# Scaling the rows of the v projection on GpSimd, with weight splits, addends and restores moved

## The reference, cut to what matters

```python
def chunk_mlp_mixer(h, w_uv, ln_gain, ln_bias, ws, bs, w_out):
    z = gelu(einsum('btd,de->bte', h, w_uv))
    u, v = z[..., :C_WIDTH], z[..., C_WIDTH:]
    v = layer_norm(v, ln_gain, ln_bias)
    ...
    mixed = einsum('gts,bnsgc->bntgc', w, vc) + bs[:, :L].T[None, None, :, :, None]
    y = u * mixed.reshape(B, T, C_WIDTH)
    return einsum('bte,ed->btd', y, w_out), v

def conv_ffn(h, conv_hist, w_in, conv_w, conv_b, w_out):
    a, gate = proj[..., :D_FF], proj[..., D_FF:]
    conv = conv_b + sum(full[:, j:j + T] * conv_w[j] for j in range(CONV_W))
    y = einsum('btf,fd->btd', gelu(conv) * gate, w_out)
```

## Time and profile before

| | |
|---|---|
| median of 3 runs | 2880.27 us |
| the profiled execution, its time | 2880.13 us |
| its span, first to last instruction | 2878.4 us |
| mean granted TensorE clock | 0.995 |
| PE busy | 2828.3 us, 98% of the span |
| DVE busy | 1494.2 us, 52% |
| ACT busy | 699.4 us, 24% |
| POOL busy | 740.2 us, 26% |
| PE in the chain that ended last | 92% |

### The profile page before, as it was taken

One profiled execution on the slowest core, in us unless ns is written; L12 is line 12 of the kernel. 1 busy time (PEld: TensorE's weight loads), 2 busy tenths in 40 slices (PEclk: granted clock), 3 DMA queues, 4 the chain that ended last, 5 costly groups with the idle time before them and its releaser, 6 DMA issues.

```text
span 2878.4 us, 44387 instructions
## 1 busy us (share of the span) xinstructions
PE 2828.3 (98%) x16227; PEld 2753.0 (96%) x16227; DVE 1494.2 (52%) x2670; ACT 699.4 (24%) x1157; POOL 740.2 (26%) x549
## 2 busy tenths in 40 slices
PE   8998999999999999999999999999999999999999
PEld 8998889999999999999888999999999999999997
DVE  4558886544444444456422765456544444444452
ACT  4423344311111111113322221214311111111123
POOL 3133334432222222222100330012422222222220
PEclk9999999999999999999999999999999999999999
DMA  4111001111111111111211111111111111111111
GB/s 144 37 33 49 23 17 41 46 42 44 40 43 41 40 43 40 44 40 45 70 44 33 60 41 40 44 40 37 48 45 40 44 40 43 40 43 41 42 53 76
DMA packets 194883, 130.72 MB, mean 45 GB/s; under 512 B 8859, under 2 KB 186724, under 8 KB 194532
## 3 DMA queue, kind: packets, MB, share of 16 engines
q1 hardware_dynamic: 194788, 129.44, 14.8%
HBM read 120.60 MB, written 8.81 MB: 45 GB/s over the span
## 4 chain that ended last, share of the span: by engine, by line
PE 92%; DVE 5%; issue 2%; ACT 1%; POOL 0%; DMA 0%; DVEq 0%; SPq 0%; ACTq 0%; POOLq 0%
PE bank L693 47%; PE bank L718 21%; PE bank L1206 7%; PE bank L742 3%; PE bank L850 3%; PE bank L1130 2%; PE bank L1317 2%; PE bank L881 1%; PE bank L792 1%; PE bank L1098 1%; PE bank L1266 1%; PE bank L1326 1%; DVE qsc L1488 1%; DVE sct L1508 1%; DVE work L1995 0%
## 5 line engine op out<-in xcount | busy, mean ns | idle before, releaser
L2730 POOL TENSOR_TENSOR raw<-raw,vec 128x512 f32<-128x512 f32 x248 | 281.2, 1145 | 1308.1 <-DMA raw<-in_w_in_ffn 845.1
L693 PE MATMUL bank<-xh,wh 128*128 128x384 f32 x2664 | 607.6, 335 | 3.1 <-DVE wl L1345 2.4
L693 PE MATMUL bank<-xl,wh 128*128 128x384 f32 x2664 | 604.5, 334 | 0.0
L693 PE MATMUL bank<-xh,wl 128*128 128x384 f32 x2664 | 604.5, 334 | 0.0
L2117 ACT ACTIVATE wh<-raw 128x512 fp32r<-128x512 f32 x374 | 235.2, 629 | 1396.6 <-PE bank L693 770.5
L1345 DVE TENSOR_TENSOR wl<-raw,wh 128x512 fp32r<-128x512 f32 x374 | 282.6, 756 | 417.7 <-ACT wh L2117 417.7
L693 PEld LDWEIGHTS bank<-xh,wh 128*128 128x128 f32 x2664 | 473.3, 188 | 6.3 <-issue 3.5
L693 PEld LDWEIGHTS bank<-xl,wh 128*128 128x128 f32 x2664 | 474.6, 188 | 0.0
L693 PEld LDWEIGHTS bank<-xh,wl 128*128 128x128 f32 x2664 | 474.5, 188 | 0.0
L1371 DVE TENSOR_TENSOR xs<-bank,xs 128x384 f32<-128x384 f32 (+1 forms) x648 | 320.8, 550 | 281.0 <-PE bank L718 246.9
L718 PE MATMUL bank<-yh,wh 128*128 128x384 f32 x1152 | 264.9, 338 | 0.0
(11 more groups left out here) (318 smaller groups left out, 3421.0 us busy)
## 6 DMA issues: line engine op xcount, KB each, us to landing
raw<-in_w_in_ffn SPq DMA_DIRECT2D x176, 256.0 KB, 2.9
raw<-in_w_out_ffn SPq DMA_DIRECT2D x88, 256.0 KB, 2.7
raw<-in_w_uv_c SPq DMA_DIRECT2D x64, 256.0 KB, 2.8
raw<-in_w_in_ab SPq DMA_DIRECT2D x40, 256.0 KB, 2.9
raw<-in_w_out_c SPq DMA_DIRECT2D x32, 256.0 KB, 2.7
xtok<-in_x_prompt SPq DMA_DIRECT2D x8, 512.0 KB, 6.3
raw<-in_w_out_ab SPq DMA_DIRECT2D x16, 256.0 KB, 2.7
out_y_prompt<-otok SPq DMA_DIRECT2D x8, 512.0 KB, 2.6
```

The costliest lines, as they stand in the source:

```text
L693: mm = pe.matmul(ps[(sg + tb) % BANKS][:, 0:TB], w[:, place, k * P:(k + 1) * P], r[:, kk, tbs(tb)], start=kk == 0 and c == 0, stop=kk == K ...
L2730: pool.tensor_tensor(r, r, g, ALU.mult).then_inc(w_scaled, 1)
```

## The change

1. The 32 v pieces are multiplied by the gain on POOL (`scale_rows`, one instruction of 128x512 each); ACT's `v_high` becomes a plain copy that waits for POOL, and DVE's `v_low` a plain subtraction.
2. In `ups` on DVE, `low` of the second piece of the second and third unit stands behind `conv_taps` rather than ahead of it.
3. `addend(0)` and `addend(1)` move behind `hold(1)` and into the first `mix_take`.
4. POOL's eight instructions on `gbc` become one of 128x2048 and two of 128x1024.
5. POOL restores `xs` without the wait for the last gated u rows (`u_gated`, 12), and DVE waits for all eight restored slices before the first `add_down` of stage `ua` rather than for one at a time.

```diff
--- before.py
+++ after.py
@@ -1346,11 +1346,9 @@
                     .then_inc(w_low_ready, 1)
 
             def v_low(n):
-                k = (n - V_N) % 8
-                hi, lo = v_place(k)
+                hi, lo = v_place((n - V_N) % 8)
                 dve.wait_ge(w_high_ready, n + 1)
-                dve.scalar_tensor_tensor(lo, raw[:, n % RAWS, :], vec[:, V_MIX + KD + k:V_MIX + KD + k + 1],
-                                         hi.bitcast(F32), ALU.mult, ALU.subtract).then_inc(w_low_ready, 1)
+                dve.tensor_tensor(lo, raw[:, n % RAWS, :], hi.bitcast(F32), ALU.subtract).then_inc(w_low_ready, 1)
 
             def fin_low(p):
                 hi, lo = fin_piece(p)
@@ -1786,12 +1784,10 @@
                     low(n0 + 2 * q + 1, n0 + 2 * q + 1)
                     if q:
                         lows(2 * q - 1)
+                    low(n0 + 2 * q + 2, n0 + 2 * q + 2)
                     if k == 2 and q == 3:
-                        v_low(V_N)
                         v_low(V_N + 1)
                         v_low(V_N + 2)
-                    else:
-                        low(n0 + 2 * q + 2, n0 + 2 * q + 2)
                     adds(2 * q)
                     lows(2 * q)
                     adds(2 * q + 1)
@@ -1858,7 +1854,7 @@
                 def ups(n, sn, g, sg, tick, s):
                     opening = isinstance(s, int) and s == 0
                     for u in range(4):
-                        if u in (0, 3):
+                        if not (u == 1 and opening):
                             low(n + 2 * u + 1, sn + 2 * u + 1)
                         if l and u == 3 and isinstance(s, int) and s:
                             for p in range(4):
@@ -1874,8 +1870,6 @@
                         if u < 2:
                             fc = 2 * s + u
                             conv_unit(u, ds(fc, 1), fc, sg + 3 * u, tk)
-                            if not (u == 0 and opening):
-                                low(n + 2 * u + 3, sn + 2 * u + 3)
                             conv_taps(u, fc, fc, g + 3 * u + 3)
                         else:
                             if some(2 * s + done0):
@@ -1966,21 +1960,21 @@
             low(n0 + 3, n0 + 3)
             for t in range(1, NT - 1 - LN_ACT):
                 normalise(t)
+            low(n0 + 4, n0 + 4)
+            hold(1)
+
+            dve.wait_ge(wsum_ready, 4)
+            dve.wait_ge(bsb_ready, 1)
+
             def addend(j):
                 if j > 1:
                     dve.wait_ge(mixed_out, 3 * (j - 1))
                 dve.scalar_tensor_tensor(adde[:, j % 2, :], wsum[:, j // 2, :], vec[:, V_LNB + j:V_LNB + j + 1],
                                          bsb[:, j // 2, :], ALU.mult, ALU.add).then_inc(addend_ready, 1)
-            dve.wait_ge(wsum_ready, 4)
-            dve.wait_ge(bsb_ready, 1)
-            addend(0)
-            addend(1)
-            low(n0 + 4, n0 + 4)
-            hold(1)
 
             def mix_take(j):
 
-                if j and j + 1 < CJ:
+                if j + 1 < CJ:
                     addend(j + 1)
                 dve.wait_ge(addend_ready, j + 1)
                 gain = vec[:, V_LNG + j:V_LNG + j + 1]
@@ -2034,6 +2028,7 @@
 
 
             na, ga, ta = PLAN.at["ua"]
+            addend(0)
             for step in range(16):
                 u, k = divmod(step, 8)
                 if step == 8:
@@ -2056,13 +2051,12 @@
                     gated_ut(1, 0, 2)
             y_low(0)
             u_groups(1, 1, ga + 3, ta + 6, lambda: low(na + 5, na + 5))
+            dve.wait_ge(xs_init, 2 * KD)
             for q in range(4):
                 if q:
                     low(na + 5 + q, na + 5 + q)
                 for m in range(6 * q, 6 * q + 6):
                     d, tb = divmod(m, NTB)
-                    if tb == 0:
-                        dve.wait_ge(xs_init, KD + d + 1)
                     add_down(d, tb, ga + 6 + m, ga + 6 + m, ta + 9 + m)
             n1, g1, t1 = PLAN.at["u"]
 
@@ -2117,12 +2111,10 @@
                 act.activation(wh[:, s % 2, :], raw[:, s % RAWS, :], ACT.Copy).then_inc(w_high_ready, 1)
 
             def v_high(n, tick):
-                k = (n - V_N) % 8
-                act.wait_ge(raw_loaded[n % RAWS], 16 * (n // RAWS + 1))
+                act.wait_ge(w_scaled, n + 1)
                 if tick:
                     act.wait_ge(pe_tick, tick)
-                act.activation(v_place(k)[0], raw[:, n % RAWS, :], ACT.Identity,
-                               scale=vec[:, V_MIX + KD + k:V_MIX + KD + k + 1]).then_inc(w_high_ready, 1)
+                act.activation(v_place((n - V_N) % 8)[0], raw[:, n % RAWS, :], ACT.Copy).then_inc(w_high_ready, 1)
 
             def fin_high(p, tick):
                 act.wait_ge(w_scaled, FIN_N + p + 1)
@@ -2482,8 +2474,8 @@
                 for q in range(4):
                     for dd in range(2):
                         p = n0 + 2 * q + dd + 2
-                        if k == 2 and q == 3:
-                            v_high(V_N + 3 * dd, t0 + (28 if dd else 22))
+                        if k == 2 and q == 3 and dd:
+                            v_high(V_N + 3, t0 + 28)
                         else:
                             high(p, p, t0 + 7 * q + (7 if dd else 1))
                         if k == 2 and q == 3 and not dd:
@@ -2728,6 +2720,13 @@
                 c = gain + 4 * (s % 2)
                 g = vec[:, c:c + 4].rearrange("p (k o) -> p k o", o=1).to_broadcast([P, 4, P])
                 pool.tensor_tensor(r, r, g, ALU.mult).then_inc(w_scaled, 1)
+
+            def scale_rows(n):
+
+                pool.wait_ge(raw_loaded[n % RAWS], 16 * (n // RAWS + 1))
+                k = V_MIX + KD + (n - V_N) % 8
+                r = raw[:, n % RAWS, :]
+                pool.tensor_tensor(r, r, vec[:, k:k + 1].to_broadcast([P, 512]), ALU.mult).then_inc(w_scaled, 1)
 
             def add_square(e, par, tb, sq, ssq):
                 pool.wait_ge(square_ready, e - 23)
@@ -2849,11 +2848,17 @@
                             scale_weights(n0 + p, 0, 4, None)
                         elif gain is not None:
                             scale_weights(n0 + p, 0, 4, gain)
+                        else:
+                            scale_rows(n0 + p)
                     if q == 3 and gain is None:
-                        pool.wait_ge(w_scaled, V_N)
-                        pool.sem_inc(w_scaled, 32)
+                        scale_rows(n0 + 10)
+                        scale_rows(n0 + 11)
                     for m in range(6 * q, 6 * q + 6):
                         add_square(24 * k + m, m % 2, m % NTB, sq_b, ssq_b)
+                        if gain is None and m == 20:
+                            scale_rows(n0 + 12)
+                            scale_rows(n0 + 13)
+                            scale_rows(n0 + 14)
 
             def ffn(l):
                 done0 = 2 * (STEPS * l + (8 if l else 0))
@@ -2908,11 +2913,14 @@
             ffn(0)
             n0, _, _ = PLAN.at["v"]
             gain = V_MIX + KD
+            scale_rows(V_N + KD - 1)
             pool.wait_ge(acc_free, PLAN.at["v"][1])
             pool.memset(wsn[:, :, :], 0.0).then_inc(wsn_zero, 1)
             pool.wait_ge(ws_loaded, 16 * 9)
 
             pool.memset(wnat[0:64, :, 64:P], 0.0).then_inc(wnat_masked, 1)
+            for n in range(V_N + KD, V_N + 32):
+                scale_rows(n)
             n0, _, _ = PLAN.at["u0"]
             for p in range(4):
                 scale_weights(n0 + p, 0, 4, gain)
@@ -2927,15 +2935,12 @@
             pool.wait_ge(gbc_loaded, 48)
             pool.wait_ge(ln_done, NT - LN_ACT)
             nv = work[:, 8:24, SEQ:TOK]
-            for b in range(4):
-                gb = gbc[:, 4 * b:4 * b + 4, :]
-                ins = pool.tensor_tensor(gb, gb, nv[:, 4 * b:4 * b + 4, :], ALU.mult)
-            ins.then_inc(v_out_used, 1)
+            pool.tensor_tensor(gbc[:, :, :], gbc[:, :, :], nv, ALU.mult).then_inc(v_out_used, 1)
             scale_weights(na + 2, 0, 4, gain)
             pool.wait_ge(v_out_used, 1)
-            for b in range(4):
-                gb = gbc[:, 4 * b:4 * b + 4, :]
-                ins = pool.tensor_tensor(gb, gb, bbc[b // 2][:, 4 * (b % 2):4 * (b % 2) + 4, :], ALU.add)
+            for b in range(2):
+                gb = gbc[:, 8 * b:8 * b + 8, :]
+                ins = pool.tensor_tensor(gb, gb, bbc[b][:, :, :], ALU.add)
             ins.then_inc(vout_ready, 1)
             scale_weights(na + 3, 0, 4, gain)
             pool.wait_ge(u_gated, 6)
@@ -2944,7 +2949,6 @@
                     for p in range(4, 8):
                         scale_weights(na + p, 0, 4, None)
                     pool.wait_ge(mixed_out, 48)
-                    pool.wait_ge(u_gated, 12)
                 pool.tensor_tensor(xs[:, k, :], xh[:, k, :].bitcast(F32), xl[:, k, :].bitcast(F32), ALU.add)\
                     .then_inc(xs_init, 1)
             n1, _, _ = PLAN.at["u"]
```

## The result

The changed kernel takes 2929.11 us (median of 4 runs, 2926.86 to 2929.97) against 2880.29 us: ratio 1.0173, 95% interval 1.0162 to 1.0184, so 48.8 us or 1.7% slower. (The 28 executions of it on record, which the ratio covers, have a median of 2930.3 us, 50.0 us slower; the four alone give 1.0170.) It lies 12 us above the forecast of 2917 us and just above the top of its range, 2929 us. The profiled execution took 2928.97 us, its span is 2927.3 us and its mean clock 0.994, where the kernel before has 0.995.

What follows compares the result with a forecast made beforehand. PE, busy 2828.3 of 2878.4 us, was taken as the bound. FFN 12.6, v start 7.4, addends and gbc 4.5, restores 10.0 and clock 2.7 sum to 37.2 us on 2880.13: 2917 us, range 2898 to 2929.

Steps and rivals of the forecast that it cites:

- What bounds it: Whole kernel: PE is busy 2828.3 us of the 2878.4 us span, so only what makes PE wait can cost.
- the rule of the held-up instruction: All stages beside POOL: DVE instructions with two SBUF operands are held up by POOL's running instruction, such as 2.65 us restores.
- The rival without it: All stages: POOL does not hold up DVE; 20.6 us slower, 2901 us, chance 0.14.
- FFN, the step that failed: Both FFNs: late `low` makes PE wait 0.43 us in second units, 0.1 us in third, plus openings; 12.6 us.
- The bounds: FFN: 3 us with a chain 0.4 us shorter, 25 us with 0.3 us more in each of 42 units.
- v start: Start of the v projection: POOL's scalings delay the pieces, PE waits 4.7 and 2.1 us; 7.4 us late.
- Addends and gbc: Stage ua: addends meet POOL's long multiplies, so PE gets the first mixing result late; 4.5 us.
- Restores: Stage ua's down: early restores alternate with DVE's work, first bank free late, PE stands after six banks; 10.0 us.
- the signs: Expected in the trace at the restores: `y_low` about 2.7 us each, first `add_down` behind the last restore, PE idle near 7 us.
- The clock: Behind the restores: one fall of PE's clock to half rate, 2.7 us; bounds 0 and 11 us.
- The rival with a fall at each new wait: At the new PE waits: four clock falls instead of one; 2925 us, chance 0.11.
- Not slower: FFN: taps starting 0.6 us earlier in 42 units give 25.2 us back; 2879.5 us, chance 0.03.

Runs made afterwards that it cites:

- edit 2 alone: The kernel before with only the FFN change, `low` of the second and third unit's second piece behind the taps: 2909.54 us against 2879.78, ratio 1.0104.
- edit 1 alone: The kernel before with only the v change, POOL scaling the 32 v pieces: 2886.48 us, 6.7 us slower, ratio 1.0022.
- edit 2 taken back: The changed kernel with the FFN `low` of the second and third unit ahead of the taps again: 2901.71 us, ratio 1.0076 against the kernel before.
- edit 5 alone: The kernel before with only the restores early and one wait for all eight slices: 2890.40 us, 10.6 us slower, ratio 1.0037.

## Why the prediction was wrong

1. *What bounds it, and the rule of the held-up instruction*: right. The rows of the changed kernel shown above fit it, from the `low` of 4.93 us beside a multiply of 4.62 us to the three PSUM readers that keep 1.49 us. The rival without it, 2901 us, is out. Its sum was also too high by its own terms: without any holding up, L1820 ends 0.4 us sooner in 20 steps and the openings lose nothing, which leaves about 2.6 us of FFN instead of 11, and 2892 us.
2. *FFN, the step that failed.* The prediction said that PE starts the second unit's second half "0.43 us late" in 20 steps and "0.1 us" in the third unit, 12.6 us in all. The runs show 0.92 and 0.50 us, 30.0 us in all (29.8 with edit 2 alone). The chain of causes was right, the openings too (38.56 us between two L1816 there, against 37.56, the 1.0 us predicted). The second unit's 0.49 us more is made up of four parts. First, the gap behind L1816 is 0.30 us in the loop and not the 0.12 us of the earlier trace rows. The earlier trace rows is from the opening step, which is unrolled; in the last, unrolled step of the changed kernel the gap is 0.10 us and the second unit loses only 0.7 and 0.8 us. The trace has a register instruction of 57 to 89 ns on DVE at L1816 in the 36 instances of the loop and in none of the eight unrolled ones; that such work fills the gap was not tested by a run of its own. This is 0.18 us. Second, PE's due time: 972.87 + 3 x 6.24 was worked out from the chain, while PE's own row for that half begins at 991.43 and not 991.59, 0.16 us. Third, from the end of `low` to the first matmul it is 0.15 us where 0.1 was allowed. Fourth, the first rows behind the restart come 0.11 us too slowly. Together 0.50 us. Each of the four was under 0.2 us, but with the 0.4 us more in the third unit, from the same causes, 20 steps made them 17 us. The bounds named this ("0.3 us more in each of 42 units", 25 us), but the range counted it as unlikely, and the measured 30.0 us lies above even that bound.
3. *v start*: the place and the mechanism were right, the size was 4.6 us for 7.4. The waits are 3.6 us before V_N+3 and twice 0.4 us. The prediction had 4.7 and 2.1, and a start of the v projection 1.0 us late: it let every DVE instruction lose its turn, while DVE itself waits for ACT between some of them (1.00 us idle before 1394.26) and lets POOL run on. POOL's three adds end at 1395.05 and its three scalings at 1398.99, which is 1379.9 and 1383.9 less the 15.1 us; the prediction had 1380.7 and 1385.2. The 24 later scalings cost nothing, as predicted: `bn_aggr` behind the v projection is 19.7 us late, as the start of it was.
4. *Addends and gbc*: 4.9 for 4.5 us, but of other parts: 3.3 us of delay where 4.5 were worked out, and about 1.5 us of half clock behind it.
5. *Restores*: 9.4 us where 10.0 and 2.7 for the clock behind them were predicted. DVE comes to its first add at 1710.66, and that add sets when PE can go on, as worked out (1687.5 predicted, 1710.66 less the 24.6 us of shift is 1686.1). The way there was not all as told: each `yl` takes 3.8 us, where the signs named 2.7. And PE was to run through six banks and then stand for 6.8 us. It stands for 2.8 us at its third result already, for a bank that still holds a product of the u unit; the prediction left that out. It lies inside the wait for the first add, so it changed nothing in the sum; that was luck.
6. *The clock*: it was expected once, for 2.7 us, behind the restores. In the profiled execution of the changed kernel it falls behind the mixing wait (1.5 us) and at 1704 to 1709 us, where PE then stands for the restores anyway. The rival with a fall at each new wait is refuted for this execution, but not as a mechanism: edit 1 alone and the kernel with edit 2 taken back fall at the v start too. The Trainium skill ("TensorE: Matmul & The Clock Gate", section "Part 1: The HAM clock gate") has the clock fall when PE has been idle; the rows above agree, all their falls lie behind waits, and they show beyond it that an equal wait of 3.6 us can leave the clock at 1.00.
7. *Not slower*: nothing came back from the taps that start earlier. PE's steps without a wait keep their pace of 0.52 us for three matmuls.

The errors partly cancel: the FFN was 17.4 us too low and the other terms together, the clock among them, 5.7 us too high, so the sum is off by 12 us only.

The parts measured alone add to 29.8 + 6.7 + 5.3 + 10.6 = 52.4 us, against 48.8 us together. The stages stand apart in time; the main difference that the traces show between a stage alone and the same stage in the changed kernel is the clock behind its wait. That it accounts for all of the 3.6 us is not shown, since each sum carries the noise of four medians, about 1 us each.

What stays open is what decides whether a wait lets the clock fall. It need not be the kernel, for the clock differs between executions of the same instructions. From 165 to 170 us, in layer 0, where no edit reaches, the mean granted clock is 1.00 in the profile of the kernel before, 0.84 in that of edit 2 alone and 0.78 in that of edit 5 alone. And the 28 executions of the changed kernel on record run from 2926.86 us at a mean clock of 0.995 to 2933.99 us at 0.991. So one profile for each kernel can't put a fall, or its absence, down to an edit.

## What to carry to other kernels

A forecast in which a small time is repeated many times needs the instruction rows of the very place, on both engines: take the releasing instruction's end and the waiting engine's due time from the loop itself and not from an opening step or a chain's average, and add the restart. Work moved ahead of the operand that the critical engine waits for costs its whole length past the slack. Long instructions on POOL are harmless only while DVE has nothing urgent with two SBUF operands. Where the median of a whole kernel can't show a delay of 1 or 2 us, the time between two fixed instructions of its trace can: here it repeated to 0.01 us where nothing had been changed between them.
